# The opening of a two-layer encoder step: x and the first weight slot loaded in pieces, the first tile by pairs of blocks

## The reference

```
h = rms_norm(x, ln_pre_mix)      # y = x * rsqrt(mean(x*x) + 1e-6) * g
y = h @ w_in                     # 1024 -> 2304, split into attention, gating and retention parts
```

## Time and profile before

| | us |
|---|---|
| median of 3 runs | 1333.43 |
| lowest and highest | 1333.14, 1333.62 |
| the profiled execution's own time | 1333.2 |
| its span, first to last instruction | 1331.1 |
| TensorE busy | 1316.8 (99%) |
| VectorE busy | 713.9 (54%) |
| ScalarE busy | 491.5 (37%) |
| GpSimd busy | 159.7 (12%) |

### The profile page before, as it was taken

The page is one execution under the profiler, slowest core; times in us unless marked ns, Lnnn a source line. Parts: engine busy times, 40 slices in busy tenths (PEclk is TensorE's granted clock), DMA queues, the critical chain, the costliest instruction groups (busy, mean ns, idle before and its releaser), DMA issues.

```text
span 1331.1 us, 22221 instructions
## 1 busy us (share of the span) xinstructions
PE 1316.8 (99%) x9412; PEld 1231.0 (92%) x9412; DVE 713.9 (54%) x1257; ACT 491.5 (37%) x1008; POOL 159.7 (12%) x214
## 2 busy tenths in 40 slices
PE   9999999999999999999999999999999999999998
PEld 9999779999999999999999996899999999999997
DVE  5656874855555555222558488566655555542223
ACT  6323475632322223222433136664432232232221
POOL 4102024400000000000340020252000000000010
PEclk9999999999999999999999999999999999999999
DMA  4512102132222222222233121031322222222212
GB/s 173 185 55 76 49 1 78 50 127 80 80 93 82 79 80 91 85 80 80 82 110 110 49 76 33 23 101 44 109 91 80 80 83 92 80 79 82 93 48 71
DMA packets 33314, 107.81 MB, mean 81 GB/s; under 512 B 4144, under 2 KB 8640, under 8 KB 33216
## 3 DMA queue, kind: packets, MB, share of 16 engines
q1 hardware_dynamic: 31056, 101.25, 23.7%
q0 software_dynamic: 2160, 5.15, 1.2%
HBM read 103.24 MB, written 3.15 MB: 80 GB/s over the span
## 4 chain that ended last, share of the span: by engine, by line
PE 95%; DVE 2%; ACT 1%; issue 1%; DMA 0%; SPq 0%; ACTq 0%; DVEq 0%
PE psum L500 21%; PE psum L502 20%; PE psum L501 20%; PE psum L511 15%; PE psum L512 8%; PE psum L510 2%; PE psum L509 1%; DVE rsq L1554 1%; PE psum L520 1%; PE psum L772 1%; PE psum L809 1%; PE psum L641 1%; PE psum L530 1%; PE psum L638 1%; PE psum L564 0%
## 5 line engine op out<-in xcount | busy, mean ns | idle before, releaser
L500 PE MATMUL psum<-h,w_hi 128*128 128x320 f32 (+1 forms) x1584 | 484.8, 306 | 0.0
L502 PE MATMUL psum<-h,w_lo 128*128 128x320 f32 (+1 forms) x1584 | 477.1, 301 | 0.0
L501 PE MATMUL psum<-h,w_hi 128*128 128x320 f32 (+1 forms) x1584 | 477.0, 301 | 0.0
L1396 DVE TENSOR_TENSOR w_lo<-raw,w_hi 128x1024 fp32r<-128x1024 f32 x184 | 227.6, 1245 | 316.5 <-ACT w_hi L1009 316.5
L500 PEld LDWEIGHTS psum<-h,w_hi 128*128 128x128 f32 x1584 | 299.1, 189 | 4.5 <-issue 1.7
L501 PEld LDWEIGHTS psum<-h,w_hi 128*128 128x128 f32 x1584 | 299.2, 189 | 3.9
L502 PEld LDWEIGHTS psum<-h,w_lo 128*128 128x128 f32 x1584 | 299.0, 189 | 0.0
L1009 ACT ACTIVATE w_hi<-raw 128x1024 fp32r<-128x1024 f32 x184 | 192.2, 1049 | 164.2 <-DMA raw<-in_wts 164.2
L511 PE MATMUL psum<-h,w_hi 128*128 128x512 f32 x532 | 191.0, 398 | 0.0
L512 PE MATMUL psum<-h,w_lo 128*128 128x256 f32 x532 | 149.4, 281 | 0.0
L1918 POOL TENSOR_TENSOR acc<-acc,sq 128x256 f32<-128x256 f32 (+1 forms) x111 | 103.8, 935 | 242.3 <-ACT sq L1009 232.9
(11 more groups left out here) (219 smaller groups left out, 1549.4 us busy)
## 6 DMA issues: line engine op xcount, KB each, us to landing
raw<-in_wts SPq DMA_DIRECT2D x184, 512.0 KB, 3.5
x<-in_xT SPq DMA_DIRECT2D x2, 640.0 KB, 10.2
tab<-in_tabs POOLq DMA_DIRECT2D x2, 640.0 KB, 5.3
lp<-in_lpar POOLq DMA_DIRECT2D x2, 640.0 KB, 5.5
out_x<-x SPq DMA_DIRECT2D x4, 320.0 KB, 2.6
tab<-in_tabs POOLq DMA_DIRECT2D x2, 577.0 KB, 4.4
x<-in_xT SPq DMA_DIRECT2D x2, 512.0 KB, 5.4
out_x<-x SPq DMA_DIRECT2D x4, 256.0 KB, 2.1
```

The source lines that it names most:

```text
L500: pe.matmul(out, wh, hi, start=first, stop=False)
L501: pe.matmul(out, wh, lo, start=False, stop=False)
L502: return pe.matmul(out, wl, hi, start=False, stop=last)
L1396: dve.tensor_tensor(w_lo[:, r, :], raw[:, r, :], w_hi[:, r, :].bitcast(F32), ALU.subtract)\
```

## The change

- SP no longer loads the small tables first. It loads x of group 0 in four pieces of two blocks and slot 0 in two halves of four blocks, in turn: piece, half, piece, half, piece, piece. ScalarE issues the small table of layer 0 as its first instruction; GpSimd issues the identity and layer 1's row, behind a wait for the third piece of x.
- The table `mask` is dropped, as an input, as a load and as a place in the memory.
- ScalarE and VectorE make x by pairs of blocks and slot 0 by halves, each as its piece lands.
- Tile 0 (`very_first`) goes by pairs of blocks and mixes the three kinds of product.
- ScalarE splits slot 4 ahead of squares 6 and 7 (it was behind them).
- The negated sinks are made at the head of each layer, with a wait for the first reader; layer 1 waits for its row of the small table.

The diff, cut:

```diff
-        mask = place("mask", [P, P + 256], BF16)
...
             def load_x(g, i):
-                ks = slice(i * KT // 2, (i + 1) * KT // 2)
+                n = KT // 2 if g else KT // 4
+                ks = slice(i * n, (i + 1) * n)
...
-            spe.dma_start(sp[:, :, :], small.rearrange("l p n -> p l n")).then_inc(small_landed, 16)
             load_x(0, 0)
-            load_slot(0)
+            spe.dma_start(raw[:, 0, 0:512], wts[0][:, 0:512]).then_inc(raw_first, 16)
             load_x(0, 1)
+            spe.dma_start(raw[:, 0, 512:1024], wts[0][:, 512:1024]).then_inc(raw_landed[0], 16)
+            load_x(0, 2)
+            load_x(0, 3)
             load_slot(1)
...
+            def very_first(out, wh, wl):
+                def hi_hi(ks):
+                    for k in ks:
+                        pe.wait_ge(hhi_ready, k + 1)
+                        pe.matmul(out, wh[:, k, :], h_hi[0][:, k, :], start=k == 0, stop=False)
+                def hi_lo(ks):
+                    for k in ks:
+                        pe.wait_ge(h_ready, k + 1)
+                        mm = pe.matmul(out, wh[:, k, :], h_lo[0][:, k, :], start=False, stop=k == KT - 1)
+                    return mm
+                def lo_hi(ks):
+                    for k in ks:
+                        pe.matmul(out, wl[:, k, :], h_hi[0][:, k, :], start=False, stop=False)
+                pe.wait_ge(hi_first, 1)
+                hi_hi((0, 1))
+                hi_lo((0, 1))
+                hi_hi((2, 3))
+                pe.wait_ge(lo_first, 1)
+                lo_hi(range(4))
+                pe.wait_ge(hi_made, 1)
+                hi_lo((2, 3))
+                hi_hi((4, 5))
+                hi_lo((4, 5))
+                hi_hi((6, 7))
+                pe.wait_ge(lo_made, 1)
+                lo_hi(range(4, KT))
+                hi_lo((6, 7)).then_inc(tile_done, 1)
...
+            act.dma_start(sp[:, 0, :], small[0]).then_inc(small_landed, 16)
...
-            for k in range(4):
-                hi_of_x(0, k, 0, "pre_mix")
-            split(0)
-            act.wait_ge(x_landed[1], 16)
-            for k in range(4, KT):
-                hi_of_x(0, k, 0, "pre_mix")
+            for i in range(KT // 2):
+                act.wait_ge(x_landed[i], 16)
+                for k in (2 * i, 2 * i + 1):
+                    hi_of_x(0, k, 0, "pre_mix")
+                if i == 0:
+                    act.wait_ge(raw_first, 16)
+                    fn(w_hi[:, 0, 0:512], raw[:, 0, 0:512], ACT.Copy).then_inc(hi_first, 1)
+                if i == 1:
+                    act.wait_ge(raw_landed[0], 16)
+                    fn(w_hi[:, 0, 512:1024], raw[:, 0, 512:1024], ACT.Copy).then_inc(hi_made, 1)
...
             split(3)
-            for k in range(4, KT):
-                first_square(k)
+            first_square(4)
+            first_square(5)
             split(4)
-            act.wait_ge(x_landed[2], 16)
+            first_square(6)
+            first_square(7)
+            act.wait_ge(x_landed[4], 16)
...
-            for k in range(4):
-                lo_of_x(0, k, 0, "pre_mix", k + 1)
-            split(0)
-            for k in range(4, KT):
+            for k in range(KT):
                 lo_of_x(0, k, 0, "pre_mix", k + 1)
+                if k in (1, 3):
+                    part = slice(256 * (k - 1), 256 * (k + 1))
+                    dve.wait_ge(*((hi_first, 1) if k == 1 else (hi_made, 1)))
+                    dve.tensor_tensor(w_lo[:, 0, part], raw[:, 0, part], w_hi[:, 0, part].bitcast(F32), ALU.subtract)\
+                       .then_inc(lo_first if k == 1 else lo_made, 1)
...
-                if l == 0:
-                    dve.wait_ge(nsink_ready, 1)
-
+                if l:
+                    dve.wait_ge(small_later, (DEPTH - 1) * 16)
+                dve.tensor_scalar(nsink[:, l, :], sp[:, l, SP["sink"]:SP["sink"] + 4], -1.0, None, ALU.mult)\
+                   .then_inc(nsink_ready, 1)
...
+            pool.wait_ge(x_landed[2], 16)
             pool.dma_start(ident[:, :], ident_d).then_inc(const_landed, 16)
-            pool.dma_start(mask[:, :], mask_d).then_inc(const_landed, 16)
+            for l in range(1, DEPTH):
+                pool.dma_start(sp[:, l, :], small[l]).then_inc(small_later, 16)
```

More of the change, by code:

```diff
@@ L155, with program @@
 EARLY = KT
-def program(nc, xT, wts, small, tabs, lpar, kcache, vcache, ret0, ident_d, mask_d,
+def program(nc, xT, wts, small, tabs, lpar, kcache, vcache, ret0, ident_d,
             o_x, o_k, o_v, o_rp, o_rs, o_gv):
@@ L316, in add_sides @@
             return dve.tensor_reduce(out, whole(i).rearrange("p (s n) -> p n s", s=2), AX.X, ALU.add)
-        x_landed = [sem(f"x_landed{i}") for i in range(4)]
+        x_landed = [sem(f"x_landed{i}") for i in range(6)]
+        raw_first = sem("raw_first")
+        hi_first = sem("hi_first")
+        lo_first = sem("lo_first")
         const_landed = sem("const_landed")
@@ L321, in program @@
         small_landed = sem("small_landed")
+        small_later = sem("small_later")
         tab_landed = sem("tab_landed")
@@ L455, in load_x @@
             def load_x(g, i):
-                ks = slice(i * KT // 2, (i + 1) * KT // 2)
-                spe.dma_start(x[:, ks, cols(g)], xT[:, ks, cols(g)]).then_inc(x_landed[2 * g + i], 16)
+                n = KT // 2 if g else KT // 4
+                ks = slice(i * n, (i + 1) * n)
+                spe.dma_start(x[:, ks, cols(g)], xT[:, ks, cols(g)]).then_inc(x_landed[4 * g + i], 16)
             def load_slot(n):
@@ L559, in first_tile @@
                 wh, wl = (w[:, n % RING, :].rearrange("p (k m) -> p k m", m=P) for w in (w_hi, w_lo))
+                if t == 0:
+                    return very_first(out, wh, wl)
                 pe.wait_ge(hi_made, n + 1)
                 for k in range(KT):
-                    if t == 0:
-                        pe.wait_ge(hhi_ready, k + 1)
                     pe.matmul(out, wh[:, k, :], h_hi[0][:, k, :], start=k == 0, stop=False)
                 for k in range(KT):
-                    if t == 0:
-                        pe.wait_ge(h_ready, k + 1)
                     pe.matmul(out, wh[:, k, :], h_lo[0][:, k, :], start=False, stop=False)
@@ L727, in _ @@
                     first_tile(4)
-                    pe.wait_ge(const_landed, 32)
+                    pe.wait_ge(const_landed, 16)
                     spread(l, "pre_mix", 0, NORM_BANK[0])
@@ L1043, in _ @@
             act.wait_ge(small_landed, 16)
-            act.wait_ge(x_landed[0], 16)
             def first_square(k, g=0):
@@ L1072, in _ @@
             root(0, "pre_mix", 0, NORM_BANK[0], D)
-            act.wait_ge(x_landed[3], 16)
+            act.wait_ge(x_landed[5], 16)
             for k in range(4, KT):
@@ L1102, in next_h @@
                     square_of(part, "pre", g, k, x[:, k, cols(g)])
+                if l:
+                    act.wait_ge(small_later, (DEPTH - 1) * 16)
                 if l == 0:
@@ L1409, in _ @@
             dve.wait_ge(small_landed, 16)
-            for l in range(DEPTH):
-                last = dve.tensor_scalar(nsink[:, l, :], sp[:, l, SP["sink"]:SP["sink"] + 4], -1.0, None, ALU.mult)
-            last.then_inc(nsink_ready, 1)
             def recip(l, name, g):
@@ L1683, in maxima @@
                     ns = nsink[:, l, :]
+                    if c == 0:
+                        dve.wait_ge(nsink_ready, L(1, 1))
                     if c >= 2:
@@ L2037 @@
     from concourse.bass_utils import run_bass_kernel_spmd
-    import ml_dtypes
     a = {k: np.asarray(v) for k, v in inputs.items()}
@@ L2077 @@
                                 .reshape(DEPTH, P, 2, HD))
-    q = np.arange(P) < CHUNK
-    keys = np.arange(256)
-    two = np.concatenate([np.stack([q, ~q]).astype(f), np.stack([keys >= 192, keys < 64]) * f(-1e30)], axis=1)
-    mask = np.zeros((P, P + 256), ml_dtypes.bfloat16)
-    mask[0:2] = two
     arrays = dict(xT=xT, wts=wts, small=small, tabs=constants(), lpar=lpar, kcache=kcache, vcache=vcache, ret0=ret0,
-                  ident=np.eye(P, dtype=f), mask=mask)
+                  ident=np.eye(P, dtype=f))
     outs = dict(x=(P, KT, T), k=(DEPTH, P, P + DEC), v=(DEPTH, P, P + DEC), rp=(DEPTH, P, 2, HD),
```

## The result

The changed kernel takes 1337.07 us in the median of 14 runs (1333.8 to 1337.56), the kernel before 1333.99 in 14 runs beside it. The ratio is 1.0017, 95% interval 1.001 to 1.0024: slower, by less than 0.2%. Its profiled execution took 1336.59 us with a span of 1334.8; the span is 3.7 us longer than before. Of its 14 executions three averaged a granted clock of 1.00 and took 1333.80 to 1334.44 us; the eleven others, at 0.996 to 0.999, took 1335.92 to 1337.56.

What follows compares the result with a forecast made beforehand. TensorE, busy 1316.8 of 1331.1 us and 95% of the chain, was taken as the bound. -1.25 at tile 0 and +0.88 at the sums gave -0.37: 1333.43 to 1333.06, given as 1333.1 us; 8-in-10 range 1332.0 to 1333.9.

Steps and rivals of the forecast that it cites:

- The start at 8.35, set by the warm-up: TensorE's first load of tile 0: its start is set by the 20 kept warm-up matmuls, not by any load.
- Tile 0 gains 1.25 us: Tile 0 on TensorE: loses its stall and ends at 11.23 in place of 12.48, called nearly certain.
- slot 1 is split by 10.3 for a tile at 11.23: Weights for tile 1: slot 1 is split well before TensorE needs it, so no wait there.
- All of x at 7.7, slot 1 at 9.2: Opening loads: x lands at about 7.7 us (bounds 7.2 and 8.67), slot 1 at about 9.2, bringing GpSimd's first operation to 10.6.
- The fourth meeting of the additions with a weight split costs 0.9 us: GpSimd's additions for the squares: VectorE's split of slot 4 collides with addition 6 or 7, 0.8 to 1.0 us, lower bound 0.
- Slot 4 lands at 16.7, bounds 16.2 and 17.4: Load of slot 4: lands at about 16.7 us in place of 17.4, by an earlier start and 96 KB less.
- slot 4 is late and holds the squares: Rival at ScalarE: squares 6 and 7 wait behind slot 4's load; sums 0.2 us later, 1333.6 us; 13 in 100.
- Everything after is released by TensorE, so it moves along: All work after the sums of squares shifts with TensorE, so the total changes by the same -0.37 us.
- The cut pieces in series: Rival in the opening loads: six pieces do not overlap, end at 15.3 us, time 1338 us; 3 in 100.
- the dropped table: Unread table in the opening loads: saves 96 KB, 0.24 us; later tables move by 768 bytes, effect a few in a hundred.
- the moved sinks: VectorE's sink product at each layer's head: hidden by 3.43 us of idling in layer 0; uncovered at most 0.24 us in all.

Runs made afterwards that it cites:

- the run with only the order: The kernel before with only ScalarE's split of slot 4 put ahead of squares 6 and 7; 1334.04 us, ratio 1.0004.
- TensorE kept busy: The changed kernel with 14 matmuls of ones by ones on TensorE ahead of its first sums; 1335.35 us, ratio to before 1.0009.
- slot 4 put back: The changed kernel with ScalarE's split of slot 4 moved back behind squares 6 and 7; 1332.88 us, ratio to the kernel before 0.999.
- slots loaded first: The changed kernel with slots 3 and 4 loaded ahead of both halves of group 1's x; 1334.56 us, ratio 1.0003.
- early squares: The changed kernel with slot 4 split behind the squares, squares made earlier, GpSimd's two table loads behind its second square; 1331.93 us, ratio 0.9986.
- early squares with slots first: The changed kernel with slot 4 split behind squares made earlier, and slots 3 and 4 loaded ahead of group 1's x; 1331.55 us, ratio 0.9986.

## Why the prediction was wrong

- *The start at 8.35, set by the warm-up.* Right here: 8.13, with the 40 loads unbroken (7.12 us). That no load sets it was luck: in the kernel before, the copy of slot 0 ended at 8.30 as well, and in the run with only the order, where the warm-up ended at 7.59, tile 0 stood 0.89 us for that copy. And the clock was misread: 40 loads in 7.12 us are 0.18 us each, while the 28 loads of the same form that filled the wait (TensorE kept busy) took 3.21 us, 0.115 each. The first part of the warm-up ran at a lower pace, although the granted clock reads 1.00 there. With it the start moves, from 7.69 to 8.49 us in the traces of the changed kernel and its variants.
- *Tile 0 gains 1.25 us.* Right in size: 1.30. The term "slot 1 is split by 10.3 for a tile at 11.23" was wrong: the copy ended at 11.13 and tile 1 began at 11.18. With slot 4 put back tile 1 waited for it, and the gain at tile 1 was 0.96.
- *All of x at 7.7, slot 1 at 9.2.* Slot 1 was copied at 10.07, on landing, 0.9 us late. The earlier issue won its half microsecond at first, and the hole in the loads at 4.5 to 6.5 us (417 KB moved there, against 790 before) lost it again. Tile 0 did not need it, tile 1 and the squares did: GpSimd began at 11.50, not 10.6.
- *The fourth meeting of the additions with a weight split costs 0.9 us.* Right in kind and near in size: 1.1 (slots loaded first). With this and the late head the forecast's own sum is 11.5 + 9.15 + 1.1 = 21.75 for the end of the squares, later than the 20.87 of before: the gain was gone without any late load.
- *Slot 4 lands at 16.7, bounds 16.2 and 17.4.* **This is the step that failed.** It took the one landing in one profile for the bound. Seen in traces here: 17.4 and 19.1 for the kernel before, 19.2, 19.4, 18.8 and 18.4 with the new order, 19.3 with early squares. The 17.4 that the prediction had to go by is the earliest of them. Nor did the earlier start carry over: SP issued slot 4 at 7.10 in the changed kernel, at 5.41 before. The rival "slot 4 is late and holds the squares" named the mechanism and the place, and was priced at +0.2 us for a landing at 17.4; at 19.4, 2 us later, the same working gives sums at 23.3, and they came at 23.26.
- *"Everything after is released by TensorE, so it moves along."* Wrong: 1.44 us of the loss is the lower clock after the idle time, a term that the sum put at nothing. I looked for the clock only as a gain. The Trainium skill (TensorE: Matmul & The Clock Gate, "Why this matters for your kernels") warns of idle gaps between bursts of matmuls. The traces agree, with 0.50 at 24 to 25 us after 3.39 us of idle time, and show the fall after 2.69 and 1.92 us too.
- *The cut pieces in series; the dropped table; the moved sinks.* No sign of the first; slot 4 put back leaves all three in and is faster than before.

Put together, the loss in the profiled execution is -1.30 at tile 0, +3.44 in the wait for the squares, +0.07 in the sums and +1.44 by the clock. The wait is 2.57 us of longer chain (11.71 us against 9.14: 1.94 of waiting for square 6, the rest of collision) on top of the 0.82 that is there with the old order. Against the forecast of -0.37 the sum is 4.02 us worse: 0.90 by the late head of the squares, 1.66 by their length (11.71 in place of 10.05), 1.44 by the clock and 0.02 in small terms.

What stays open is why slot 4's landing moves by 1.7 us between two executions of one program. The Trainium skill (DMA: Bandwidth & Descriptors, "Why a DMA increments its semaphore by 16 and not by 1") says that a transfer's parts run on up to 16 engines that finish independently, and the semaphore counts all of them; a straggler would look like the 25 GB/s at a DMA share of 0.07 at 18.5 us. No view read here shows which engine was last, or why.

## What to carry to other kernels

A consumer placed behind everything else hides how widely its load lands; before it is moved ahead of work that others wait for, its landing is to be read in several executions, and the slack of the old place is part of its price. When a stall is mended, the next chain must be followed by its head and its length both: here the squares came forward by 0.2 us and had to come by 1.0. And the cost of a wait on TensorE does not end with the wait, since the clock may fall behind it.

## What was not expected of the hardware

The lower clock came after the idle time was over. After 3.39 us of idle time the clock was down within half a microsecond. After 2.69 and 1.92 us it fell 1.3 and 1.6 us after TensorE had begun again (0.52 at 23 to 24 us with slots first). After 1.82 us, in the kernel with only the order changed, it did not fall at all; these are single executions, and 1.82 and 1.92 are close. Once down it stayed there for 3 to 4 us with TensorE fully busy.

The changed kernel's runs spread over 3.8 us, of which two were traced. The moving landing and this clock can account for a part only. The kernel before, which does not wait for slot 4, spreads over 3.5 us beside it (1333.04 to 1336.57), and in the traced execution of early squares with slots first the granted clock reads 0.50 from 161 to 164 us, far behind the edit. Why the clock falls there in some executions and not in others is not shown.
